# First attention on one core: the transposes of the step behind move ahead of the product's four k-tiles

## The chip, the cores and the metric

The kernel is one program on 1 core of a Trainium2 chip. Six instruction streams run side by side: TensorE (PE, whose weight loads the profile shows apart as PEld), VectorE (DVE), ScalarE (ACT), GpSimd (POOL), SyncE (SP) and the DMA queues that they start. They meet only at semaphores. The metric is the device time of one execution in microseconds; lower is better. All times below are us unless marked otherwise.

## What is computed

A hidden state of 512 tokens by 1024 features goes through a first block of two layers (a gated MLP with a feed-forward, then a banded attention with a feed-forward) and a second block (feed-forward, sparse attention and retention merged, feed-forward, a gate). The change lies in the banded attention, called first attention here. Cut to what matters:

```python
q = (h @ w_q).reshape(bsz, nc, CHUNK, ATTN_HEADS, HEAD_DIM)       # 16 heads of 64
s = jnp.einsum('bcqhd,bckhd->bchqk', q, k_band)
s = s * (HEAD_DIM ** -0.5) + relative_bias(rel_table)[None, None]
s = jnp.where(valid[None, :, None, None, :], s, NEG_INF)          # own chunk and the 8 before it
p = jax.nn.softmax(s, axis=-1)
o = jnp.einsum('bchqk,bckhd->bcqhd', p, v_band).reshape(bsz, seq, D_MODEL)
return o @ w_o
```

## The kernel before

**Products.** Everything is held feature-major in tiles of 128 partitions, in fp32, and each large matrix product is made of three passes of a value split into a high and a low part: high weights by high input (L349), high weights by low input (L350), low weights by high input (L351). One k-tile of one product is three matmuls of 128x512. Weights come in units of 128x1024. SP loads a unit into one of four slots of RAW; POOL splits it into WH (L309) and then WL (L312); TensorE multiplies with it. POOL may overwrite the WH of a slot only when TensorE has counted the unit that used it as done (`units_done`), so the last k-tile of a product releases POOL's next two instructions. Both instructions read and write SBUF only.

**The first attention.** Eight pairs of heads (p = 0 to 7), each with four query tiles (t = 0 to 3) of 128 tokens: 32 steps s = 4p + t. Query tile t sees n = 128(t+1) keys. A step has three parts on TensorE, for the two heads (hh = 0, 1) of the pair:

- `pair_scores(s)` (L556): four matmuls in all. It waits until the scores of the step before are read (`x_done`).
- `pair_transposes(s)` (L566): t+1 transposes for each head, of the probabilities PROB. Those of a head wait for the normalised probabilities of that head (`p_done`).
- `pair_values(s)` (L577): the product of the transposed probabilities PROBT with the values, (t+1) times two.

Between these parts TensorE works on "fillers", each one k-tile of a product: `filler(j)` for j below 128 is k-tile j%8 of unit j//8 of the sixteen K and Q products of the coming pairs, and from 128 on a k-tile of the output projection (L519, L520, L526). Eighteen fillers run ahead of the loop and four in every step: step s has j = 18 + 4s to 21 + 4s. So in even steps the four are k-tiles 2 to 5 of a unit. In odd steps (t = 1 and t = 3) they are k-tiles 6 and 7, which end a unit, and k-tiles 0 and 1 of the next.

**The other engines, in their order.** VectorE in step s: for both heads, bias and maximum (`tensor_tensor_reduce`, L1374, scores from PSUM); then at t = 1 the taking out of a K tile (`take_k`, L1347, which waits for the unit that ends in this step) and the low part of the output of the pair before (`low_output`, L1359); at t = 3 the taking out of a Q tile (`take_q`, L1352, which waits in the same way); then for each head the reciprocal of the sum (L1387) and the normalisation of PROB in place (L1388, `tensor_scalar`, SBUF to SBUF), which counts `p_done`. ScalarE in step s: PROBT of step s-1 out of PSUM for both heads (`probs_out`, L929, after the transposes), then the exponentials of step s for both heads (L943, after L1374). Each engine runs its instructions in this order: one that waits holds up all that stand behind it.

The sparse attention of the second block (L666 to L696, L1494 to L1505) has the same parts with one filler in place of each two: scores, filler, transposes, filler, values.

Of the kernel before, what the change touches and what calls it, by code (L numbers as in the profile page):

```python
# [117 lines left out]
def program(nc, xT, weights, gains, cols, lng, lnb, bs, wsT, rel, pos, ident_d, decay, pT, out):  # L118
    with ExitStack() as ctx:
# [204 lines left out]
        def _(pe):  # L324
# [176 lines left out]
            def kq_tile(j):  # L501

                n, k = kq0 + j // DT, j % DT
                xh, xl = (XH, XL) if n % 2 == 0 else (HH, HL)
                if k == 0:
                    pe.wait_ge(weights_split, n + 1 + SLOTS)
                    pe.wait_ge(evacuated, n + 3)
                last = three_passes(2 + n % 2, n % SLOTS, slice(k * P, k * P + P), xh, xl, k, k == DT - 1)
                if k == DT - 1:
                    last.then_inc(units_done, 1)  # L510
# [18 lines left out]
            def out_tile(j):  # L529

                n, k = (out0 + j % 2, j // 2) if j < 2 * DT - 2 else (out0 + 2, j - 2 * DT + 2)
                if k == 0:
                    pe.wait_ge(weights_split, n + 1 + SLOTS)
                    pe.wait_ge(evacuated, n + 1 if n != out0 + 1 else out0 + SLOTS)
                    if n == out0 + 2:
                        pe.wait_ge(o_low, DT - 1)
                pe.wait_ge(o_low, k + 1)
                out_high(n, k)
                out_low(n, k)

            def filler(j):

                if j < 2 * DT * DT:
                    kq_tile(j)
                elif j < 2 * DT * DT + 3 * (DT - 1):
                    out_tile(j - 2 * DT * DT)

            def pair_scores(s):
                p, t = divmod(s, TT)
                if t == 0:  # L550
                    pe.wait_ge(evacuated, kq0 + 2 * p + 2 + SLOTS)
                if s:
                    pe.wait_ge(x_done, 2 * s)
                for hh in range(2):
                    r = slice(hh * HD, hh * HD + HD)
                    nc.tensor.matmul(PS[:, 4 + hh, 0:n_of(t)], KQ[r, 2 + p % 2, t * P:t * P + P],  # L556
                                     KQ[r, p % 2, 0:n_of(t)], start=True, stop=True).then_inc(s_done2, 1)

            def pair_transposes(s):
                t = s % TT  # L560
                for hh in range(2):
                    pe.wait_ge(p_done, 2 * s + hh + 1)
                    if s:
                        pe.wait_ge(pt_done, 2 * s - 1 + hh)
                    for k in range(t + 1):
                        last = nc.tensor.transpose(PS[:, 6 + hh, k * P:k * P + P],  # L566
                                                   PROB[:, s % 2, hh, k * P:k * P + P], IDENT[:])
                    last.then_inc(t_done2, 1)

            def pair_values(s):  # L570
                p, t = divmod(s, TT)
                pe.wait_ge(pt_done, 2 * s + 2)
                if t == 0 and p >= 2:
                    pe.wait_ge(o_low, p - 1)
                for k in range(t + 1):
                    for hh in range(2):
                        last = nc.tensor.matmul(PS[hh * HD:hh * HD + HD, p % 2, t * P:t * P + P],  # L577
                                                VT[:, k, (2 * p + hh) * HD:(2 * p + hh) * HD + HD],
                                                PROBT[:, hh, k * P:k * P + P], start=(k == 0), stop=(k == t))
                        if k == t:  # L580
                            last.then_inc(pv_done2, 1)
# [4 lines left out]
            for s in range(steps + 1):  # L586
                j = 2 * DT + 2 + 4 * s
                if s < steps:
                    pair_scores(s)
                filler(j)  # L590
                filler(j + 1)
                if s:
                    pair_transposes(s - 1)
                filler(j + 2)
                filler(j + 3)
                if s:
                    pair_values(s - 1)
            pe.wait_ge(o_high, DT)
# [1136 lines left out]
```

## Time and profile before

| | us |
|---|---|
| median of 3 executions | 2535.15 |
| lowest, highest | 2534.99, 2538.76 |
| the profiled execution, its own time | 2538.28 |
| its span, from the first to the last instruction | 2536.5 |
| PE, PEld busy | 2413.1 (95%), 1944.4 (77%) |
| DVE, ACT, POOL busy | 1223.5 (48%), 506.6 (20%), 1760.5 (69%) |
| mean granted TensorE clock, as a share of full speed | 0.978 |
| the loop over the 32 steps | from 627 to 792 in the span |

Busy shares are means over stages with different limits. TensorE's matmuls overlap in the records, so that a stretch shown as full may hold short gaps; a gap that lasts shows as idle time with the name of what ended it. PEld instructions lie beside the matmuls of PE.

### The profile page before, as it was taken

The page shows a single profiled execution, that of the slowest core. Times are in us where ns is not written, and L with a number is a line of the kernel's source. Part 1 is how long each engine was busy: PE and PEld are TensorE (multiplying, and loading weights), DVE is VectorE, ACT ScalarE, POOL GpSimd, SP SyncE. Part 2 cuts the span into 40 slices and gives each one's busy share as a digit, 9 for nine tenths or more (in the row PEclk, how much of TensorE's full clock was granted, in tenths as well). Part 3 has the DMA queues.
Part 4 walks back from the last instruction along what each step waited for, and adds up shares of the span by engine and source line. Part 5 has one row for each costly group of instructions (what it writes and reads, how often), then busy time and mean ns, then how long its engine had stood idle before and what let it go on. Part 6 is the DMA issues. An engine that isn't in the chain of part 4 may idle for free.

```text
span 2536.5 us, 31074 instructions
## 1 busy us (share of the span) xinstructions
PE 2413.1 (95%) x11054; PEld 1944.4 (77%) x11054; DVE 1223.5 (48%) x1649; ACT 506.6 (20%) x931; POOL 1760.5 (69%) x827
## 2 busy tenths in 40 slices
PE   7789999998999899999999999998899999999998
PEld 6677888876667788887888887676588877888876
DVE  3656324444664633436534236588664342333365
ACT  2122001121342300112201001420432121110022
POOL 7656877865445587786788876665238886887865
PEclk9899999999999999999999999998999999999999
DMA  5222333323222233333233332232113332333322
GB/s 185 74 75 67 100 99 91 99 83 90 74 74 67 67 104 95 91 103 92 75 108 93 98 89 85 75 100 67 30 38 91 100 95 71 107 99 92 92 81 75
DMA packets 64806, 221.57 MB, mean 87 GB/s; under 512 B 7504, under 2 KB 9680, under 8 KB 64592
## 3 DMA queue, kind: packets, MB, share of 16 engines
q1 hardware_dynamic: 59184, 208.17, 27.7%
q10 hardware_dynamic: 5536, 12.19, 1.5%
q8 instruction: 61, 1.00, 0.2%
q14 instruction: 25, 0.20, 0.0%
HBM read 218.23 MB, written 2.10 MB: 87 GB/s over the span
## 4 chain that ended last, share of the span: by engine, by line
PE 83%; DVE 8%; POOL 4%; issue 3%; ACT 2%; ACTq 0%; DVEq 0%; POOLq 0%
PE PS L349 24%; PE PS L350 23%; PE PS L351 23%; PE PS L409 4%; POOL WH L309 2%; POOL WL L312 2%; PE PS L556 1%; PE PS L577 1%; PE PS L566 1%; PE PS L710 1%; PE PS L519 1%; ACT PS L973 1%; DVE PROB L1505 1%; PE PS L526 1%; PE PS L520 1%
## 5 line engine op out<-in xcount | busy, mean ns | idle before, releaser
L309 POOL TENSOR_TENSOR WH<-RAW,ONES 128x1024 fp32r<-128x1024 f32 (+3 forms) x411 | 781.5, 1902 | 721.1 <-PE PS L351 634.0
L312 POOL TENSOR_TENSOR WL<-RAW,WH 128x1024 fp32r<-128x1024 f32 (+3 forms) x411 | 984.5, 2395 | 32.3
L349 PE MATMUL PS<-XH,WH 128*128 128x512 f32 x1816 | 726.8, 400 | 49.5 <-POOL WL L312 22.9
L350 PE MATMUL PS<-XL,WH 128*128 128x512 f32 x1816 | 713.5, 393 | 0.0
L351 PE MATMUL PS<-XH,WL 128*128 128x512 f32 x1816 | 712.8, 393 | 0.0
L349 PEld LDWEIGHTS PS<-XH,WH 128*128 128x128 f32 x1816 | 345.0, 190 | 143.0 <-issue 33.0
L351 PEld LDWEIGHTS PS<-XH,WL 128*128 128x128 f32 x1816 | 345.0, 190 | 73.7
L350 PEld LDWEIGHTS PS<-XL,WH 128*128 128x128 f32 x1816 | 345.6, 190 | 67.7
L349 PE MATMUL PS<-HH,WH 128*128 128x512 f32 x992 | 389.4, 393 | 4.5 <-POOL WL L312 1.9
L351 PE MATMUL PS<-HH,WL 128*128 128x512 f32 x992 | 386.2, 389 | 0.0
L350 PE MATMUL PS<-HL,WH 128*128 128x512 f32 x992 | 386.2, 389 | 0.0
L1191 DVE TENSOR_TENSOR HL<-T,HH 128x512 f32 x108 | 231.1, 2140 | 152.2 <-ACT HH L856 107.8
L349 PEld LDWEIGHTS PS<-HH,WH 128*128 128x128 f32 x992 | 186.2, 188 | 53.4 <-issue 9.1
L351 PEld LDWEIGHTS PS<-HH,WL 128*128 128x128 f32 x992 | 186.2, 188 | 39.1
L350 PEld LDWEIGHTS PS<-HL,WH 128*128 128x128 f32 x992 | 186.3, 188 | 37.5
L1221 DVE TENSOR_TENSOR M<-PS,M 128x512 f32 x80 | 55.0, 692 | 311.0 <-PE PS L351 310.3
L853 ACT ACTIVATE T<-T 128x512 f32<-128x512 f32 x64 | 40.4, 632 | 485.5 <-DVE T L1198 485.5
L1208 DVE TENSOR_TENSOR T<-PS,RI 128x512 f32<-128x512 f32 x44 | 30.4, 690 | 185.2 <-PE PS L351 185.2
L409 PE MATMUL PS<-WH,XH 128*128 128x512 f32 x192 | 80.2, 417 | 29.7 <-DVE XL L1125 18.1
L1125 DVE SCALAR_TENSOR_TENSOR XL<-H,GAIN,XH 128x512 fp32r<-128x512 f32 x64 | 86.2, 1346 | 12.8 <-ACT XH L880 11.2
L864 ACT ACTIVATE T<-T 128x512 f32<-128x512 f32 x44 | 27.8, 632 | 273.6 <-DVE T L1206 273.6
L868 ACT ACTIVATE HH<-T 128x512 f32 x44 | 27.8, 633 | 270.4 <-DVE T L1211 270.4
(200 smaller groups left out, 2252.6 us busy)
## 6 DMA issues: line engine op xcount, KB each, us to landing
RAW<-in_weights SPq DMA_DIRECT2D x379, 512.0 KB, 3.5
RAW<-in_weights SPq DMA_DIRECT2D x16, 384.0 KB, 3.1
H<-in_xT ACTq DMA_DIRECT2D x8, 256.0 KB, 8.4
BIAS<-in_rel ACTq DMA_DIRECT2D x8, 256.0 KB, 3.4
RAW<-in_weights SPq DMA_DIRECT2D x8, 256.0 KB, 2.6
out<-R ACTq DMA_DIRECT2D x8, 256.0 KB, 2.2
BIAS<-in_rel ACTq DMA_DIRECT2D x8, 224.0 KB, 3.7
DECAY<-in_decay ACTq DMA_DIRECT2D x1, 1024.0 KB, 4.9
```

The lines of the kernel that those rows point to most:

```text
L309: nc.gpsimd.tensor_tensor(WH[:, slot, 0:w], raw, ONES[:, 0:1].to_broadcast([P, w]), ALU.mult).then_inc(high_split, 1)
L312: nc.gpsimd.tensor_tensor(WL[:, slot, 0:w], raw, WH[:, slot, 0:w].bitcast(F32), ALU.subtract).then_inc(weights_split, 1)
L349: nc.tensor.matmul(PS[:, bank_, :], WH[:, slot, w], xh[:, k, :], start=(k == 0), stop=False)
L350: nc.tensor.matmul(PS[:, bank_, :], WH[:, slot, w], xl[:, k, :], start=False, stop=False)
L351: return nc.tensor.matmul(PS[:, bank_, :], WL[:, slot, w], xh[:, k, :], start=False, stop=stop)
L409: last = nc.tensor.matmul(PS[:, (first + j) % SLOTS, :], x[:, k, tok], wt[:, slot, w], start=(k == 0 and n == 0), stop=(k == DT - 1 and n ...
L853: S.activation(T[:, 1, :], T[:, 0, :], ACT.Square).then_inc(act_self, 1)
L864: S.activation(T[:, 1, :], T[:, 0, :], ACT.Silu).then_inc(act_out, 1)
L1125: V.scalar_tensor_tensor(dl[:, t, :], H[:, t, :], gain(g, t), dh[:, t, :].bitcast(F32), ALU.mult, ALU.subtract).then_inc(ready, 1)
L1191: V.tensor_tensor(HL[:, f, :], T[:, src:src + 1, :], HH[:, f, :].bitcast(F32), ALU.subtract).then_inc(h_ready, 1)
L1208: V.tensor_tensor(T[:, 3, :], src, RI[:], ALU.mult).then_inc(evacuated, 1)
L1221: V.tensor_tensor(M[:, f, :], PS[:, slot:slot + 1, :], M[:, f, :], ALU.add)\
```

## The change

In each step of the first attention the four fillers stand together, behind the transposes of the step before and ahead of its values. Before, two stood ahead of the transposes and two behind. Nothing else is edited: the same instructions, the same waits, the same buffers.

```diff
@@ -587,12 +587,10 @@
                 j = 2 * DT + 2 + 4 * s
                 if s < steps:
                     pair_scores(s)
-                filler(j)
-                filler(j + 1)
                 if s:
                     pair_transposes(s - 1)
-                filler(j + 2)
-                filler(j + 3)
+                for k in range(j, j + 4):
+                    filler(k)
                 if s:
                     pair_values(s - 1)
             pe.wait_ge(o_high, DT)
```

## Rows read from the trace of the kernel before

**Rows 1.** The page, part 4: the chain that ended last, by engine.
```profile
PE 83%; DVE 8%; POOL 4%; issue 3%; ACT 2%; ACTq 0%; DVEq 0%; POOLq 0%
```

**Rows 2.** Busy time by stretch: length, PE, PEld, DVE, ACT, POOL, PEclk, DMA share, GB/s.
```profile
700.00:720.00 20.00, 19.99 (x124) 13.62 (x123) 13.82 (x35) 7.84 (x26) 8.55 (x4) 1.00 0.25 75
```

**Rows 3.** Waits from 620 to 800: who waited for whom, us, times, longest.
```profile
POOL WH L309 <- PE PS L351: 82.6, 16, 6.3
...
PEld PS L566 <- DVE PROB L1388: 5.4, 21, 0.3
```

**Rows 4.** The chain in order of time, one pair's four steps: start, us, what.
```profile
706.69 0.42 PE PS L556 x4
...
716.12 0.37 PE PS L577 x4
716.48 0.85 PE PS L556 x4
...
721.57 1.06 PE PS L556 x4
...
724.21 0.66 PE PS L566 x6
...
726.25 0.81 PE PS L577 x12
727.06 0.42 PE PS L556 x4
```

**Rows 5.** Timeline behind a unit's end, t = 1: start, us, engine, line [idle before].
```profile
714.58 1.89 POOL L309 TENSOR_TENSOR WH<-RAW,ONES 128x1024 fp32r<-128x1024 f32 x1 [6.31 <-PE PS L351]
...
715.15 0.68 DVE L1359 TENSOR_TENSOR OL<-PS,OH 128x512 fp32r<-128x512 f32 x1
...
715.93 0.69 DVE L1388 TENSOR_SCALAR PROB<-PROB,RECX 128x256 f32<-128x256 f32 x1
...
716.56 2.38 POOL L312 TENSOR_TENSOR WL<-RAW,WH 128x1024 fp32r<-128x1024 f32 x1
...
716.73 2.35 DVE L1388 TENSOR_SCALAR PROB<-PROB,RECX 128x256 f32<-128x256 f32 x1
...
719.14 0.20 PEld L566 LDWEIGHTS PS<-IDENT,PROB 128*128 128x128 f32 x2 [0.25 <-DVE PROB L1388]
```

**Rows 6.** The same behind a unit's end at t = 3.
```profile
703.93 1.89 POOL L309 TENSOR_TENSOR WH<-RAW,ONES 128x1024 fp32r<-128x1024 f32 x1 [5.35 <-PE PS L351]
...
704.96 0.72 ACT L943 ACTIVATE PROB<-PROB,NMX 128x512 f32<-128x512 f32 x1
...
705.90 2.38 POOL L312 TENSOR_TENSOR WL<-RAW,WH 128x1024 fp32r<-128x1024 f32 x1
...
706.01 2.55 DVE L1388 TENSOR_SCALAR PROB<-PROB,RECX 128x512 f32<-128x512 f32 x1
```

**Rows 7.** L1388 with POOL idle (timeline, last pair), and grouped by shape, 640 to 760.
```profile
776.91 0.35 DVE L1388 TENSOR_SCALAR PROB<-PROB,RECX 128x256 f32<-128x256 f32 x1
...
L1388 DVE TENSOR_SCALAR PROB<-PROB,RECX 128x512 f32<-128x512 f32 x12 | 18.2, 1518 | 0.4
```

**Rows 8.** The sparse attention: its transposes' long waits, on TensorE's timeline.
```profile
1798.40 0.66 PE L682 MATMUL PS<-IDENT,PROB 128*128 128x128 f32 x4 [1.83 <-DVE PROB L1505]
...
1801.40 0.50 PE L349 MATMUL PS<-XH,WH 128*128 128x512 f32 x1
...
1815.30 1.12 PE L682 MATMUL PS<-IDENT,PROB 128*128 128x128 f32 x4 [1.83 <-DVE PROB L1505]
...
1820.68 0.79 PE L349 MATMUL PS<-XH,WH 128*128 128x512 f32 x1
```

**Rows 9.** Stretches around those waits, columns as in Rows 2.
```profile
1775.00:1805.00 30.00, 25.91 (x180) 16.63 (x178) 21.29 (x61) 14.41 (x44) 8.60 (x4) 1.00 0.09 27
...
1814.60:1818.00 3.40, 2.70 (x11) 1.96 (x13) 2.17 (x9) 1.36 (x5) 0.36 (x1) 0.52 0.51 136
...
1835.00:1838.40 3.40, 3.40 (x10) 2.14 (x10) 1.21 (x3) 0.60 (x1) 0.00 (x0) 0.53 0.55 157
```

## Prediction

> **What bounds the kernel now.** I read the page's chain first: 83% of the time lies on TensorE [rows 1]. Then the stretches: inside the loop TensorE is busy 19.99 of 20 us with the clock at full speed, while VectorE has 13.8, ScalarE 7.8, POOL 8.6 [rows 2]. So this stage costs what TensorE's stream takes, and the others matter only where TensorE waits for them. The waits show one such place: the transposes (L566) wait 5.4 us in 21 pieces, 0.3 at most, for the normalisation (L1388) [rows 3]. Last the chain in order of time: one pair takes 706.69 to 727.06, 20.37 us [rows 4], and repeats with that period.
>
> What matters is why those waits exist at all. A lone normalisation of 128x256 takes 0.35 [rows 7]. Behind the end of a unit it takes 0.69 and then 2.35 [rows 5], or 2.55 for 128x512 [rows 6]. Over 640 to 760 the twelve calls of 128x512 average 1.52 us, so this comes back in every pair [rows 7]. The long ones end with a POOL instruction. In [rows 5] the first ends at 716.62, just behind the end of L309 at 716.47, and the second at 719.08, just behind the end of L312 at 718.94. In [rows 6] L312 ends at 708.28 and the normalisation at 708.56. I read this as a hold: a normalisation that starts while POOL works waits until that POOL instruction ends, and then takes 0.14 (128x256) to 0.28 (128x512) more. POOL starts when TensorE ends a unit: it waited for that 16 times [rows 3], 14 of them in the loop, once in each step with t = 1 or 3 up to s = 27. Today two fillers ahead of the transposes cover almost all of the hold. The change takes that cover away.
>
> **The part moved: the wait behind a unit's end.** Call the start of L309 zero. L312 starts at 1.97 and ends at 4.36 [rows 5]. The unit's last matmul ends at -0.1 (values start at 716.12 [rows 4]; less two fillers and two transposes, 1.4 + 0.2, that is 714.5).
>
> Step t = 1. VectorE waits for the unit's end in `take_k`, so its order behind zero stays: `low_output` at 0.57, normalisation of head 0 at 1.35, held by L309 to 2.04; head 1 at 2.15, held by L312 to 4.50; TensorE takes the transposes of head 1 up at 4.56 [rows 5]. Nothing ahead of zero that the change moves is late for this. On TensorE, after the change, two fillers follow the unit's end (1.4, as between 724.87 and 726.25), then values (0.37) and scores of t = 2 (0.85) [rows 4], and then at once the transposes: they start at about 2.5 and would end at 2.97 (six take 0.66, so four 0.44 [rows 4]). Head 0 is ready, head 1 is not: it goes at 4.56 and the next matmul at about 5.0. **Stall: 2.0 us.**
>
> Step t = 3. Here the change moves something ahead: the transposes of t = 2 now come before the unit's end, 1.4 + 0.66 earlier than the exponential that follows them on ScalarE needs (it starts at 704.96, 1.03 after zero [rows 6]). So the exponentials no longer delay VectorE; `take_q`, which waits for the unit's end, does. It ends near 0.57, as `take_k` does before the row at 715.15 [rows 5]. Head 0's normalisation then starts at about 0.8, in L309 (until 1.89), and by the 0.28 above ends at 2.2. Head 1 needs its reciprocal (0.2) and starts at 2.3. L312 started at 1.97 [rows 6]. It is held to 4.36 + 0.28 = 4.6. So the hold moves from head 0 to head 1, but its end stays where it was (today head 0 ends at 4.63). TensorE: -0.1 + 1.4 + values 0.81 + scores of t = 0 0.42 [rows 4] gives transposes from 2.5 to 3.4 (eight of 0.11); with head 1's four taken up at 4.7 the next matmul comes at 5.3, allowing 0.2 for the restart. **Stall: 1.9 us.**
>
> The even steps have no unit's end. Between the transposes that waited and the next ones lie four fillers, values and scores, as today, only in another order; today's 21 waits are three in each of seven pairs, all behind a unit's end [rows 3, 5], so those next transposes find their input ready on the same distance. The stall isn't paid back there either: TensorE is full.
>
> **Sum of the stalls.** 7 x 2.0 + 7 x 1.9 = 27.3. The last pair has no K or Q products left and no stall. The 5.4 us of today's waits [rows 3] are inside these and go: -5.4.
>
> **Order of the instructions.** Two fillers take 1.58 behind scores (722.63 to 724.21) and 1.38 behind transposes (724.87 to 726.25) [rows 4]. After the change transposes follow scores, for which this trace has no row. Bounds: the 0.2 goes (-6.2 over 31 steps), or the transposes inherit it and lose 0.1 more, since their first weight load no longer lies under a 512-column matmul (+3.1). I take -1.5, the middle, since the loss behind scores most likely stays with what follows them. At the ends: in s = 32 values wait for PROBT behind three fillers, not one, a few tenths, counted as nothing. DMAs are issued 14 times at most 2 us later and had POOL idle for 5.35 and 6.31 before a unit [rows 5, 6]: hidden; it would take a delay of that size to show. POOL's and SP's queues are moved past nothing.
>
> **The clock.** In the sparse attention the same wait exists, 1.83 us between the heads' transposes. Over 1775 to 1805, which holds the first two of them, the clock stayed at 1.00 (2.4 GHz) [rows 8, 9]. Behind the one at 1815.30 it fell to half (1.2 GHz), and behind the last it is 0.53 over 1835.0 to 1838.4 [rows 9]. What TensorE had done before was alike: small matmuls and a wait. So two of four. Price: from the wait to the second filler 3.00 us at full clock (1798.40 to 1801.40) and 5.38 at half (1815.30 to 1820.68) [rows 8]: 0.44 lost for each us at half. A fall as long as the short one, 3.4 us, costs 1.5. For 14 stalls: bounds none (0) and all (21), estimate 7 x 1.5 = 10.5.
>
> Here a rule of the Trainium skill stands against me: "TensorE: Matmul & The Clock Gate", section "HAM oscillation — how this bites in real kernels", ties the drop to idle gaps longer than any of these stalls. By it the clock term is nothing and the sum is the one without it. The trace does not agree: 1.83 us of waiting was followed by half clock.
>
> On the hold, "SBUF — State Buffer", section "SBUF: two separate sides", says that GpSimd and VectorE share a port pair as an exclusive lock for the whole instruction, so that POOL's L312 would wait for the normalisation let in before it. By the rule each stall grows by 0.1 to 0.2, the sum by 2. The rows show L312 starting 0.09 after L309's end with a normalisation running [rows 5]; I add nothing.
>
> **The sum.** 2538.28 (profiled execution, span 2536.5 and 1.8 around it) - 5.4 + 27.3 - 1.5 = 2558.7, and + 10.5 = 2569.2. That execution lies 3.1 above the median of 2535.15, so for a median: **2566**, +31. Its own range, from 3 to 11 falls with half of either end of the order term: 2557 to 2574.
>
> **Rivals.**
> - **The clock holds.** The fillers after each stall are dense 512-column matmuls, in the sparse attention only half as many stand there. Then 2558.7 - 3.1 = 2556, with the ends of the order term 2551 to 2560. For it: two of four waits did no harm. Against: the two that did.
> - **Only t = 1 collides.** If L309 held nothing, at t = 3 head 0 would be normalised from 0.8 to 1.3 and head 1 from 1.5 to 2.0, ahead of or just at L312. Then +14.0 - 5.4 - 1.5 + 3.5 x 1.5 = +12.4: 2548. Against it: the 0.69 for 0.35 ending at L309's end [rows 5].
> - **Faster.** The normalisation of head 1 slips in between L309 and L312. The deciding point is its start against 1.97; in [rows 5] it comes 0.17 late. What makes it early: nothing in VectorE's queue at t = 1, but the exponentials are done earlier at both t. If it did in both steps, no stall is left and today's waits go too: -5.4 - 1.5 = 2528. Unlikely, since VectorE waits at the unit's end in either step.
> - **Nothing to measure.** The change moves only order on an engine that is full, and the stalls come out as small as today's, because the records of L1388 overstate the hold. Then within 5 of 2535. Against: TensorE took the transposes up only 0.06 after the end of that record [rows 5].
>
> **Chances.** My forecast 0.57; the clock holds 0.18; only t = 1 0.11; faster 0.08; nothing 0.06. About 0.2% (5 us) is what a measurement of this kernel can tell from no change. Slower 0.86, within 0.06, faster 0.08. The range reaches over the first three with what their terms allow: 2546 to 2579; its upper end is all fourteen falls; it leaves out the last two and a little at either end.
>
> **What would show it.** The waits should list L566 for L1388 with some 27 us, 14 of them near 2 us, in every step with t = 0 and 2 from s = 2 to 28; L1388 at 128x512 should be long for head 1, not head 0; a pair should take about 23.4 us at full clock; stretches inside the loop should show PE near 18 of 20 and PEclk below 1 in some. If the long waits are there but 7 in number, the t = 3 walk is wrong. If L1388 is never near 2.4 us, the hold is. If the stalls are there and the clock stays at 1.00, the clock term is.

## Result: slower by 1.1%, and the profile after

| | before | after |
|---|---|---|
| median, us | 2536.86 | 2567.24 |
| lowest, highest | 2534.99, 2538.76 | 2562.14, 2569.8 |
| ratio, with its 95% interval | | 1.0112 (1.0096 to 1.0127) |
| profiled execution, its span | 2538.28, 2536.5 | 2562.14, 2560.4 |
| first to last weight load of the values (L577) in the loop | 634.6 to 791.8 | 634.4 to 816.3 |

Four executions of each are in the table; the median of 2535.15 ahead of the prediction is that of the first three. 2566 was forecast. The loop of the first attention takes 181.9 in place of 157.2, 24.7 more; the two profiled executions differ by 23.9. So what the change costs lies in the loop.

The page's chain, which had DVE at 8% [rows 1], now has it at 10%:

```profile
PE 81%; DVE 10%; POOL 4%; issue 3%; ACT 2%; DMA 0%; DVEq 0%; ACTq 0%; POOLq 0%
```

The stretches, columns as in [rows 2]. TensorE, full before, is busy 16.7 of 20 us in the two stretches shown and 17.3 of 20 on average from 640 to 760. The second stretch has the clock at 0.91:

```profile
680.00:700.00 20.00, 16.71 (x106) 11.47 (x101) 13.68 (x31) 7.01 (x21) 8.54 (x4) 1.00 0.19 53
...
740.00:760.00 20.00, 16.72 (x97) 11.91 (x96) 12.06 (x29) 6.67 (x22) 8.54 (x4) 0.91 0.21 54
```

The waits from 620 to 825, which answer to [rows 3] (the normalisation has moved from L1388 to L1386, two lines up, like all behind the edit):

```profile
POOL WH L309 <- PE PS L351: 106.8, 16, 8.9
...
PEld PS L566 <- DVE PROB L1386: 29.9, 22, 1.9
...
PE PS L566 <- DVE PROB L1386: 22.5, 14, 1.7
```

The weight loads of the transposes wait 29.9 us where they waited 5.4. The third line is the same waits seen from the matmuls, so it isn't added; it counts the long ones: 14, one behind each unit's end.

The chain in order of time over one pair, which answers to [rows 4] and [rows 5]:

```profile
703.59 0.63 PE PS L556 x4
704.22 0.37 PE PS L566 x2
...
706.02 0.69 DVE KQ L1345
706.71 0.60 DVE OL L1357
...
707.41 0.69 DVE PROB L1386
...
708.22 2.33 DVE PROB L1386
...
710.59 0.44 PE PS L566 x2
...
714.37 1.06 PE PS L556 x4
715.43 0.81 PE PS L566 x6
...
717.65 0.69 DVE KQ L1350
...
718.44 1.43 DVE PROB L1386
...
719.98 2.39 DVE PROB L1386
...
722.41 0.66 PE PS L566 x4
...
726.85 0.63 PE PS L556 x4
```

What to see: in the pair of [rows 4] this chain never left TensorE. Now it leaves it twice in each pair, at the unit's end: to the taking out of K or Q, to the normalisation of head 0, to the long one of head 1, and back to the transposes of head 1. From the scores of t = 1 (703.59) to those of t = 3 (714.37) it is 10.78 us, from there to the next scores of t = 1 (726.85) 12.48, together 23.26, where a pair took 20.37.

The same around the stall at t = 3 on the timeline, which answers to [rows 6]:

```profile
717.69 1.90 POOL L309 TENSOR_TENSOR WH<-RAW,ONES 128x1024 fp32r<-128x1024 f32 x1 [7.31 <-PE PS L351]
...
718.44 1.43 DVE L1386 TENSOR_SCALAR PROB<-PROB,RECX 128x512 f32<-128x512 f32 x1
...
719.67 2.41 POOL L312 TENSOR_TENSOR WL<-RAW,WH 128x1024 fp32r<-128x1024 f32 x1
...
719.98 2.38 DVE L1386 TENSOR_SCALAR PROB<-PROB,RECX 128x512 f32<-128x512 f32 x1
720.12 0.42 PEld L566 LDWEIGHTS PS<-IDENT,PROB 128*128 128x128 f32 x4
...
722.41 0.42 PEld L566 LDWEIGHTS PS<-IDENT,PROB 128*128 128x128 f32 x4 [1.86 <-DVE PROB L1386]
```

Head 0's normalisation ends at 719.87, behind L309's 719.59; head 1's at 722.36, behind L312's 722.08. Head 0's transposes go at 720.12; the weight load of head 1's waits 1.86. POOL itself is not delayed: L312 starts at 719.67, 0.08 behind the end of L309, while head 0's normalisation still runs. So VectorE and POOL do not meet only at semaphores, as the opening has it of all engines: nothing in the program ties the normalisation to L309 or L312, and it still ends with them.

### The profile page after: what moved, and what is told of

Its sections match the earlier page's. It is cut to its first block, busy times and chain, and to the rows that moved or that the text cites. A ratio compares the mean times of both kernels' runs of the same rounds, so it can differ in the third digit from the quotient of the medians.

```text
span 2560.4 us, 31074 instructions
## 1 busy us (share of the span) xinstructions
PE 2413.6 (94%) x11054; PEld 1947.8 (76%) x11054; DVE 1228.5 (48%) x1649; ACT 506.7 (20%) x931; POOL 1761.3 (69%) x827
## 4 chain that ended last, share of the span: by engine, by line
PE 81%; DVE 10%; POOL 4%; issue 3%; ACT 2%; DMA 0%; DVEq 0%; ACTq 0%; POOLq 0%
PE PS L349 23%; PE PS L351 23%; PE PS L350 23%; PE PS L409 4%; POOL WH L309 2%; DVE PROB L1386 2%; POOL WL L312 2%; PE PS L566 1%; PE PS L708 1%; DVE PROB L1503 1%; PE PS L556 1%; PE PS L519 1%; PE PS L526 1%; PE PS L577 1%; PE PS L520 1%
## 5 line engine op out<-in xcount | busy, mean ns | idle before, releaser
L309 POOL TENSOR_TENSOR WH<-RAW,ONES 128x1024 fp32r<-128x1024 f32 (+3 forms) x411 | 782.4, 1904 | 744.2 <-PE PS L351 657.0
L312 POOL TENSOR_TENSOR WL<-RAW,WH 128x1024 fp32r<-128x1024 f32 (+3 forms) x411 | 984.7, 2396 | 32.2
```

The source lines that it names most:

```text
L309: nc.gpsimd.tensor_tensor(WH[:, slot, 0:w], raw, ONES[:, 0:1].to_broadcast([P, w]), ALU.mult).then_inc(high_split, 1)
L312: nc.gpsimd.tensor_tensor(WL[:, slot, 0:w], raw, WH[:, slot, 0:w].bitcast(F32), ALU.subtract).then_inc(weights_split, 1)
```

## Experiments

All times are medians, each beside executions of the kernel before on the same chip. The 25 executions of the kernel before on one chip lie between 2532.7 and 2541.0: the seven with a mean granted clock of 0.981 average 2534.3, the eight with 0.978 average 2538.9. That scatter is larger than several of the effects below, so the period of one pair in the loop, from the chain of each profile, is the sharper number. It comes from one profiled execution each. The periods are in one table behind the experiments.

### Take the hold away, in the new order: smaller POOL instructions

Of the 16 units that POOL splits during the loop it splits 64 of 1024 columns, in both instructions. The kernel leaves out the rest of these weights, so its products there are not those of the reference; TensorE, VectorE and ScalarE run the same instructions.

```diff
+            n_full = (FIRST["att_kq"] + SLOTS) // 4
+            n_small = 2 * DT // 4
+            plan[0:1] = [(n_full, plan[0][1]), (n_small, [64] * 4), (plan[0][0] - n_full - n_small, plan[0][1])]
```

> The full change, but for the units that POOL splits while the first attention runs (units 100 to 115) both POOL instructions split only the first 64 of the 1024 columns of a unit; the rest of these weights is left as it was, so this part of the products is not that of the reference. TensorE, VectorE and ScalarE run the same instructions. My theory (the hold): no normalisation takes over 0.5 us, no transposes wait, the clock does not fall in the loop: 2537 - 5.4 - 1.5 = 2530. Rival (the chain scores, maximum, exponential, normalisation is too long by itself for transposes that stand right behind the next scores): the stalls stay, 2555 to 2567.

Measured: 2534.66, ratio 0.9994 (0.9984 to 1.0003). The period is 19.55 and TensorE is full. The median is 4.7 above the 2530 expected, and by itself it can't be told from the kernel before; the loop of the profile went from 157.2 to 151.6. So the stalls are gone, and some 3.4 us that the median lacks must lie outside the loop, where they are not explained (the mean clock of the ten executions was 0.976 to 0.979). All that the transposes (L570 here) wait for the normalisation (L1390) is this:

```profile
PEld PS L570 <- DVE PROB L1390: 3.3, 6, 0.5
```

It is idle time of the weight loads alone; the matmuls list no such wait. With the normalisation on ScalarE, below, the same six pieces stand (L567 for L948) and the period is the same:

```profile
PEld PS L567 <- ACT PROB L948: 3.3, 6, 0.5
```

So the chain of scores, maximum, exponential and normalisation is short enough by itself, and the stalls are POOL's. That rival falls.

### Which of POOL's two instructions

The same with L309 in full and only L312 cut to 64 columns, so that the kernel leaves out most of the low parts of these weights.

> The full change, with POOL's L309 (high parts) in full and its L312 (low parts) cut to 64 of 1024 columns for units 100 to 115, so that the low parts of these weights are not those of the reference. It takes the two POOL instructions apart. My theory: at t = 1 and t = 3 head 0's normalisation is still held by L309 (0.69 and 1.4), head 1's is short, since the hold that reached it was L312's; the transposes find head 1 at 2.5 to 2.8 behind L309's start, where they want it at 2.5 to 2.9: no stall over 0.3. Period 19.6 to 19.8, time 2532 to 2536, no falls inside the loop. Rival (L309 alone makes stalls of 1 us and more, the whole chain being late): 2545 or more.

Measured: 2532.46, ratio 0.9981 (0.9972 to 0.9991), period 19.55. The timeline behind a unit's end (L314 is L309, L318 is L312, L1392 the normalisation):

```profile
704.28 1.89 POOL L314 TENSOR_TENSOR WH<-RAW,ONES 128x1024 fp32r<-128x1024 f32 x1 [7.49 <-PE PS L357]
...
705.03 1.42 DVE L1392 TENSOR_SCALAR PROB<-PROB,RECX 128x512 f32<-128x512 f32 x1
706.25 0.38 POOL L318 TENSOR_TENSOR WL<-RAW,WH 128x64 fp32r<-128x64 f32 x1
...
706.57 0.48 DVE L1392 TENSOR_SCALAR PROB<-PROB,RECX 128x512 f32<-128x512 f32 x1
706.72 0.86 PEld L572 LDWEIGHTS PS<-IDENT,PROB 128*128 128x128 f32 x8
```

L309 holds head 0 (1.42, where 0.48 is the time of head 1 beside it), and nobody waits for that. Take L312 away and head 1 takes 0.48. The stall is L312's alone, as the walk of both steps said.

### Keep POOL, move the normalisation to ScalarE

```diff
-                    link(V.reciprocal(RECX[:, c:c + 1], SUMX[:, c:c + 1]))
-                    V.tensor_scalar(x, x, RECX[:, c:c + 1], None, ALU.mult).then_inc(p_done, 1)
+                    V.reciprocal(RECX[:, c:c + 1], SUMX[:, c:c + 1]).then_inc(r_done, 1)
...
+                for hh in range(2):
+                    act.wait_ge(r_done, 2 * s + hh + 1)
+                    S.activation(x, x, ACT.Copy, scale=RECX[:, c:c + 1]).then_inc(p_done, 1)
```

> The full change with the normalisation of PROB moved from VectorE to ScalarE (activation Copy with the reciprocal as scale, behind the two exponentials of the step); POOL works in full. My theory (only VectorE is held by POOL): at t = 1 the reciprocals are there 1.2 behind L309's start, the two normalisations on ScalarE end near 2.3, transposes are wanted at 2.5: no stall, 2530. Rival (POOL holds ScalarE as well): stalls stay, 2560 or more. Rival (ScalarE becomes late): waits of some tenths at each step, 2535 to 2545.

Measured, in the new order: 2532.88, ratio 0.9984 (0.9974 to 0.9993), period 19.55. The median is 2.9 above the 2530 expected; the loop is 5.5 shorter than that of the kernel before (151.7 against 157.2). POOL works in full, ScalarE is busy 12 of 20 us, and no transposes wait for VectorE. POOL does not hold ScalarE. At t = 3 head 0's normalisation (L948 here) starts when L309 (L310 here) has 1.15 to go, and takes 0.72; head 1's, most of it beside L309 too, takes 0.71. On the timeline:

```profile
701.86 1.90 POOL L310 TENSOR_TENSOR WH<-RAW,ONES 128x1024 fp32r<-128x1024 f32 x1 [5.41 <-PE PS L352]
...
702.61 0.72 ACT L948 ACTIVATE PROB<-PROB,RECX 128x512 f32<-128x512 f32 x1 [0.22 <-DVE RECX L1391]
703.24 0.71 ACT L948 ACTIVATE PROB<-PROB,RECX 128x512 f32<-128x512 f32 x1
```

And from the chain of this kernel, which shows what the same steps take without a stall (scores are L557 here, transposes L567):

```profile
698.53 1.06 PE PS L557 x4
...
704.36 1.02 PE PS L567 x8
...
709.16 0.63 PE PS L557 x4
...
718.09 1.06 PE PS L557 x4
```

From scores of t = 1 to scores of t = 3 it is 8.93 (10.78 in the changed kernel), from t = 3 to t = 1 it is 10.63 (12.48). So each of the two stalls of a pair costs 1.85.

The old order with the same edit is the fourth cell of the square:

> The kernel before in its old order, with the normalisation of first attention on ScalarE. With norm_act it shows what the order costs once nothing is held. Theory: nothing, the two periods without stalls are the same (19.6), so as norm_act: 2533, within 2. Rival (the order has a price or a gain of its own, up to 0.2 a step): 2527 or 2539.

Measured: 2533.02, ratio 0.9985 (0.9976 to 0.9995). Medians can't tell the two orders apart, their periods can. Transposes of t = 1 in the chain, old order:

```profile
697.48 0.44 PE PS L567 x4
...
717.30 0.44 PE PS L567 x4
```

That is 19.82 against 19.55. The new order is worth 0.27 a pair by itself. The chains show where most of it comes from: in the old order the first matmul of a filler behind scores takes 0.43 where the others take 0.23; in the new one it takes 0.23, but the transposes, now behind scores, take 0.15 more (0.59 for four, 0.44 above). That leaves 0.05 a step. And the old order's waits cost 20.37 - 19.82 = 0.55 a pair.

### One part of the change alone

```diff
-                for k in range(j, j + 4):
+                ahead = 0 if s % 2 == 0 else 2
+                for k in range(j, j + ahead):
                     filler(k)
                 if s:
                     pair_transposes(s - 1)
+                for k in range(j + ahead, j + 4):
+                    filler(k)
```

> The new order only in steps with t = 0 and 2, the old one in steps with t = 1 and 3. My theory (a hold of VectorE's normalisation by POOL behind a unit's end, which lies in odd steps and is met by the transposes of the next, even step): all of the loss is here. At t = 2 the stall is 2.0 as in the full change. At t = 0 it is larger, 2.5, since with the old order at t = 3 the exponentials are late, the hold falls on head 0 and head 1 follows at 5.28 behind L309's start. 7 x 4.5 - 5.4 = +26, and the clock's falls, some 8: about 2570, a little above the full change's 2567. Rival (each transposition next to scores costs something, in any step): half of the loss, 2552.

Measured: 2558.33, ratio 1.0082 (1.0065 to 1.0098), period 23.03, no fall of the clock in the loop. The expectation was 2570. The place was right, two numbers were not. At t = 0 the chain shows one block:

```profile
717.60 2.53 DVE PROB L1389
...
720.17 1.25 PE PS L566 x8
```

Eight transposes with their inputs there take 1.02 (704.36, in the chain of the kernel with ScalarE). Head 1's normalisation (0.5) runs beside head 0's transposes, so it adds 0.2 and not the 0.6 that I put. And of the eight falls none came in the loop of the profiled execution.

The other half, `ahead = 0 if s % 2 else 2`:

> The new order only in steps with t = 1 and 3. My theory: no stall, since the transposes moved there read normalisations that no POOL instruction holds. The exponentials of t = 3 come earlier, so the hold moves from head 0 to head 1 and the wait of head 0, 0.35 in each of seven pairs, goes; with 0.05 less for the order in 15 steps: 2537 - 2.4 - 0.8 = 2534, clock as before. Rival (any step costs): 2552. Rival (nothing): 2537.

Measured: 2540.7, ratio 1.0016 (1.0006 to 1.0026), period 20.61 and the loop 1.7 longer. All three expectations are off, mine by its sign. The waits:

```profile
PEld PS L566 <- DVE PROB L1389: 12.5, 22, 0.8
```

They are up from 5.4, though both fillers still stand ahead of the transposes that wait. The matmuls, which listed no such wait before, now wait 3.0 us in 13 pieces. What I had missed: the transposes of the step before stood between the unit's end and the next transposes, 0.22 us (t = 0) or 0.66 (t = 2) of cover of their own. Moved ahead of the unit's end they cover nothing. In the full change this is inside the walk, which counts only what follows the unit's end.

### How the cover prices the hold

One filler ahead in even steps, none in odd ones (`ahead = 1 if s % 2 == 0 else 0`):

> The new order, but in steps with t = 0 and 2 one filler stands ahead of the transposes and three behind. One filler is 0.7 us of cover, so each of the 14 stalls of 2.0 and 1.9 shrinks by 0.7: period 23.3 - 1.4 = 21.9, and no or few falls of the clock: 2537 + 7 x 1.5 = 2547 to 2551. Rival (the stall is set by something that moves along with the transposes): no change from 2567.

Measured: 2548.26, ratio 1.0044 (1.0027 to 1.0061), period 21.94, no falls in the loop: as expected.

Three ahead in even steps, two in odd ones:

> The kernel before, but in steps with t = 0 and 2 three fillers stand ahead of the transposes and one behind: 0.7 us more of cover than before. Theory: the waits of the transposes for the normalisation (5.4 us in all) go, and values wait for PROBT instead, 0.2 to 0.3 in each of these steps, since one filler is little for ScalarE's two copies: 2537 - 5.4 + 3.5 = 2535. Rival (one filler is enough): 2531. Rival (too little): 2540.

Measured: 2535.03, ratio 0.9999 (0.9988 to 1.001), period 19.94. The waits for the normalisation are gone and these have come:

```profile
PEld PS L577 <- ACT PROBT L930: 7.2, 16, 1.0
```

Values now wait for ScalarE's copy: the same cover, taken from the other end. These runs differ in the order of the odd steps too, so the price of cover is read within one order. With the new order in odd steps, none, one and two fillers ahead in even steps give 23.26, 21.94 and 20.61: 1.32 and 1.33 a pair for one filler in each of two steps, 0.66 a filler, nearly the 0.7 that it takes. With the old order in odd steps none, two and three give 23.03, 20.37 and 19.94: the third is worth only 0.43, since by then little hold is left to cover. Without any hold the old order takes 19.82.

### The clock

```diff
+                    if hh and t % 2 and s < 4 * (DT - 1):
+                        n = kq0 + (2 * DT + 6 + 4 * s) // DT
+                        for _ in range(6):
+                            nc.tensor.matmul(PS[:, 7, :], WH[:, n % SLOTS, 0:P], XH[:, 0, :], start=True, stop=True)
                     pe.wait_ge(p_done, 2 * s + hh + 1)
```

> The full change, and in each of the 14 places where TensorE waits for the second head's normalisation it first runs six more matmuls of 128x512 (1.4 us, into the bank that the transposes then overwrite), which lie inside the wait of 1.9. Output as before. Theory of the clock term (an idle TensorE after small matmuls is what lets the clock fall): no falls inside the loop, the period of a pair stays 23.3, time 2537 + 20 = 2557. Rival (the Trainium skill's rule on long idle gaps; the clock costs nothing here): as the changed kernel, 2567, or a little more. Rival (the extra matmuls push the transposes back): the period grows by some tenths, 2560 with no falls.

> The changed kernel once more, on the chip of the next three and with another phase of the clock's falls. The first look had three falls to half clock inside the loop and 2562, its other executions 2566 to 2570. If falls explain that spread, this profile lies at 2557.5 + 1.5 per fall inside the loop: 2562 with three, 2568 with seven. If not, time and number of falls do not go together.

Measured: the changed kernel again 2563.24, ratio 1.0101 (1.0084 to 1.0118), its profile 2561.61 with three falls, at the same places as the first. With the matmuls in the waits: 2555.82, ratio 1.0075 (1.0056 to 1.0094), period 23.35 and no falls. Its profile, 640 to 760, with the clock at 1.00, where the changed kernel has 0.96:

```profile
640.00:760.00 120.00, 117.21 (x699) 82.86 (x698) 74.99 (x182) 43.35 (x131) 43.92 (x21) 1.00 0.23 66
```

The loop takes 177.7 against 181.9, 4.2 less, though TensorE does more work and the period is 0.09 longer (0.6 in seven pairs). So three falls cost 4.8 us, 1.6 each. The chain of the changed kernel says the same: a stretch from scores to scores with a fall in it takes 12.36, 14.09 and 14.06 us, without one 10.78, 12.48 and 12.48. Each of the three falls begins within 0.6 us of the end of a stall, behind the third, fourth and tenth of the 14; those are the same three in both profiles of the changed kernel. The tenth in the chain, behind the stall that ends at 745.67, between the scores of t = 3 and the next of t = 1:

```profile
737.63 1.06 PE PS L556 x4
...
746.33 0.41 PE PS L349
...
747.16 0.43 PE PS L351
...
749.72 0.25 PE PS L351
...
751.69 0.63 PE PS L556 x4
```

0.43 for a matmul that takes 0.23 at 2.4 GHz: for eight of them the clock was at 1.2 GHz.

### A version that beats both

The sparse attention has the same hold ([rows 8]). With both normalisations on ScalarE:

> As norm_act, and the sparse attention's normalisation moved to ScalarE in the same way. The sparse attention of the kernel before waits four times 1.83 and some tenths beside, and loses two falls of the clock (6.8 and 3.4 us at half, 0.44 lost for each): 7.3 + 1.5 + 4.5 = 13 less than norm_act's 2533: 2520. Rival (with one filler where first attention has two, ScalarE has too little time for copies, exponentials and normalisations): new waits of the transposes for ScalarE, gain of a few us only, 2528 to 2535.

Measured: 2522.85, ratio 0.9939 (0.992 to 0.9957), 2.9 above the 2520 expected. The transposes of the sparse attention waited 10.7 us for VectorE (first line, the kernel before) and wait 1.3 for ScalarE, and the two falls of the clock behind those waits are gone from the profile:

```profile
PEld PS L682 <- DVE PROB L1505: 10.7, 8, 2.1
```

```profile
PEld PS L682 <- ACT PROB L1025: 1.3, 6, 0.3
```

### The periods in one table

| kernel | period of a pair | falls in the loop of its profile | time |
|---|---|---|---|
| before | 20.37 | 0 | 2536.9 |
| changed (two profiles) | 23.26 | 3 and 3 | 2567.2, 2563.2 |
| order in even steps only | 23.03 | 0 | 2558.3 |
| order in odd steps only | 20.61 | 0 | 2540.7 |
| one filler ahead | 21.94 | 0 | 2548.3 |
| three ahead in even steps | 19.94 | 0 | 2535.0 |
| changed, matmuls in the waits | 23.35 | 0 | 2555.8 |
| changed, POOL small | 19.55 | 0 | 2534.7 |
| changed, only L312 small | 19.55 | 0 | 2532.5 |
| changed, normalisation on ScalarE | 19.55 | 0 | 2532.9 |
| before, normalisation on ScalarE | 19.82 | 0 | 2533.0 |

## Why the prediction was right, and where its terms were off

**The bound and the place.** Right. TensorE sets the stage, the 14 long waits lie in steps with t = 0 and 2, seven each, where they were put. Two ways of taking the hold away, on POOL's side and on VectorE's, each leave no stall.

**The stall at t = 1.** 2.0 was put, 1.85 is what it costs (10.78 - 8.93). Head 1's normalisation starts 2.15 behind L309 and ends at 4.50 in [rows 5]; the changed chain has the same 0.69 and 2.33 behind the same taking out of K.

**The stall at t = 3.** 1.9 was put, 1.85 is what it costs (12.48 - 10.63). The step with a real move in it, hold from head 0 to head 1 with the end unchanged, came out as told: 1.43 and 2.38 on the timeline, head 1 taken up 4.72 behind L309's start where 4.7 was put.

**The sum of a pair.** From the square of order and hold: stalls 23.26 - 19.55 = 3.71 where 3.9 was put; today's waits -0.55 where -0.77 was put (5.4 in seven pairs); the order -0.27 where -0.2 was put. Together +2.89, where the steps gave +2.9: small misses that cancel. The term for today's waits was mis-sized: the 5.4 were idle time of the weight loads, and 0.55 in place of 0.77 a pair was lost to the matmuls, which still had the one in front to run. That last reason is argued, not shown. In seven pairs the sum is 20.2.

**The clock.** This is the term that was off: three falls, not seven, at 1.6 each (1.5 was put), 4.8 in place of 10.5. 20.2 + 4.8 = 25.0; the last pair, which has the new order and no stall, and the end of the loop take 0.3 less, which gives the loop's 24.7. For the profiled execution the forecast was +31 and the result +23.9, and this term is 5.7 of the 7.1 between them. Half of all stalls was read from four in the sparse attention; the loop had three in fourteen, and the kernel with the order in even steps had none in fourteen waits that were little shorter (20.2 us on the matmuls in all, against 22.5). What tells the harmless ones from the others the runs do not show; chance of a single execution it is not, since the same three stalls had a fall behind them in both profiles. The share of one half had no more behind it than four waits, and that the three falls lie inside the range, at the edge of its 3 to 11, owes something to luck. The sum without any clock term was wrong as well: falls are there, and they go when the waits are filled.

**The medians.** Over four executions the changed kernel has 2567.24, over the next four 2563.24, with both profiled ones near 2562. The mean granted clock of the first four executions goes some way with their times: 0.976 at 2562.14 (the profiled one), 0.976 at 2566.13, 0.975 at 2568.36, 0.974 at 2569.8. A fall like those above takes about 0.0007 off that mean, so the slowest may have had three falls more, anywhere in the kernel. That is an estimate from rounded numbers, and what the spread is made of stays open. So that 2566 came within 1.2 of 2567.2 is partly luck: for the profiled execution 2569.2 was about 7 too high.

**Rivals.** "The clock holds" lies nearer to the profile than my forecast did (2558.7 for that execution, against 2562.14 and 2569.2). "Only t = 1 collides" falls by the timeline: L309 does hold. "Faster" falls too: head 1's normalisation came 0.3 behind L312's start at t = 3 (719.98 against 719.67). That POOL might be held in its turn by the normalisation, for which the prediction added nothing, is not seen: L312 started 0.08 behind L309. "Nothing to measure" falls.

## What to carry to other kernels

Work that stands between two parts of a chain is cover, and what it covers may be set by an engine that neither part names: follow the longest instruction of the releasing engine to what ends with it. Count the cover from the event that starts the hold, here the end of a weight unit, and count everything that stands behind it, the moved instructions too. Where cover is dear, take the hold away: the same work on an engine that isn't held gave more than any order of the fillers.

## What the runs showed of the hardware

In these kernels a VectorE `tensor_scalar` from SBUF to SBUF (fp32, 128x256 or 128x512) that started while a POOL `tensor_tensor` of 128x1024 ran ended 0.14 to 0.28 behind it: 0.35 became up to 2.36, 0.49 up to 2.55. The POOL instruction behind it started on time (0.08 later). VectorE's reciprocals of one column (0.15, and 0.16 with POOL idle) and its `tensor_tensor` with one input in PSUM (L1357, 0.68, and 0.69 with POOL idle) ran beside POOL in their usual time, and ScalarE's activation from SBUF to SBUF was not held (0.72 for 128x512). TensorE's clock fell to half for 3.4 us behind three of fourteen waits of about 1.6 us between matmuls (22.5 in 14), at 1.6 us each, and in the profiled execution it kept full speed where 1.4 us of each wait were filled with matmuls.
